# A rotation stage that sums its squares with tokens on partitions, inverts 128x32 roots and turns them back

## What is computed

```
def rms_norm(x, w):
    xf = x.astype(jnp.float32)
    y = xf * lax.rsqrt(jnp.mean(xf * xf, axis=-1, keepdims=True) + EPS)
    return (y * w.astype(jnp.float32)).astype(x.dtype)
...
    out = jnp.concatenate([x1 * cos - x2 * sin, x2 * cos + x1 * sin], axis=-1)
...
        q = rope(rms_norm(q.reshape(B, S, N_HEADS, HEAD_DIM), q_norm_w[l]), pos)
        k = rope(rms_norm(k.reshape(B, S, N_KV_HEADS, HEAD_DIM), k_norm_w[l]), pos)
```

## Time and profile before

| what | value |
|---|---|
| median of 3 runs | 3251.81 us (3251.74 to 3253.85) |
| the profiled execution's own time | 3248.22 us |
| its span in the trace | 3246.2 us |
| TensorE busy (PE) | 3004.8 us, 93% |
| weight loads (PEld, beside PE) | 2370.2 us, 73% |
| VectorE (DVE) | 2255.4 us, 69% |
| ScalarE (ACT) | 1640.5 us, 51% |
| mean granted clock of TensorE | 0.976 of full speed |
| the stage of the change | 1774.7 to 2310.6 us |

### The profile page before, as it was taken

How to read it: one execution, slowest core, us unless ns; L and a number is a source line. 1 busy time by engine, 2 the same in 40 slices (tenths; PEclk the granted TensorE clock), 3 DMA queues, 4 the chain that set the end, 5 groups by cost and what they waited for, 6 DMA issues and landing times. The chain is left out here.

```text
span 3246.2 us, 48173 instructions
## 1 busy us (share of the span) xinstructions
PE 3004.8 (93%) x17460; PEld 2370.2 (73%) x17460; DVE 2255.4 (69%) x3296; ACT 1640.5 (51%) x3004; POOL 195.0 (6%) x448
## 2 busy tenths in 40 slices
PE   6999999999998989999999999999777889998799
PEld 5888788888787767777777778776655666776587
DVE  8888877754667758888876645324378789988543
ACT  5443422233545437777778232112377788888400
POOL 0000000000000000110000000000022111212100
PEclk8999999999999999999999999999889999999899
DMA  4444422245566541111155343223721111011665
GB/s 119 117 115 124 138 70 65 85 143 160 149 201 212 177 135 37 50 31 31 44 166 170 87 130 107 94 84 100 191 46 33 27 24 24 21 37 44 151 189 156
DMA packets 377861, 331.48 MB, mean 102 GB/s; under 512 B 100989, under 2 KB 331901, under 8 KB 371473
## 3 DMA queue, kind: packets, MB, share of 16 engines
q1 hardware_dynamic: 371640, 292.35, 31.7%
q0 software_dynamic: 5264, 35.72, 3.0%
q10 hardware_dynamic: 720, 0.31, 0.0%
HBM read 211.26 MB, written 107.10 MB: 98 GB/s over the span
## 5 line engine op out<-in xcount | busy, mean ns | idle before, releaser
L629 PE MATMUL p_oa_acc<-s_h_a_hi,s_mx_w_hi 128*128 128x512 f32 x768 | 301.7, 393 | 15.8 <-DVE s_h_a_lo L418 9.4
L323 ACT ACTIVATE s_mx_w_hi<-s_mx_raw 128x512 fp32r<-128x512 f32 x224 | 139.0, 629 | 320.6 <-PE p_oa_acc L629 256.8
L629 PE MATMUL p_oa_acc<-s_h_a_lo,s_mx_w_hi 128*128 128x512 f32 x768 | 300.0, 391 | 0.0
L629 PE MATMUL p_oa_acc<-s_h_a_hi,s_mx_w_lo 128*128 128x512 f32 x768 | 299.9, 390 | 0.0
L1598 DVE TENSOR_TENSOR_SCAN s_st_prod<-s_st_soft,s_st_prod 128x512 f32<-128x512 f32 x192 | 234.4, 1268 | 15.8 <-ACT s_st_soft L1525 15.8
L3123 PE MATMUL p_sa_turn<-s_ident,s_sa_arg 128*128 128x128 f32 x1088 | 167.4, 290 | 58.6 <-ACT s_sa_prob L2751 34.9
L1525 ACT ACTIVATE s_st_soft<-p_st_z 128x512 f32<-128x512 f32 (+3 forms) x320 | 153.7, 534 | 111.0 <-PE p_st_z L1650 111.0
L2340 PE MATMUL p_pr_ps<-s_h_hi,s_pr_w_hi 128*128 128x512 f32 (+1 forms) x712 | 195.0, 394 | 10.6 <-ACT s_pr_stage L2187 8.8
L3123 PEld LDWEIGHTS p_sa_turn<-s_ident,s_sa_arg 128*128 128x128 f32 x1088 | 120.7, 145 | 100.1 <-issue 61.7
L460 DVE TENSOR_TENSOR s_mx_w_lo<-s_mx_raw,s_mx_w_hi 128x512 fp32r<-128x512 f32 x224 | 153.4, 685 | 57.7 <-ACT s_mx_w_hi L323 56.1
L2340 PE MATMUL p_pr_ps<-s_h_lo,s_pr_w_hi 128*128 128x512 f32 (+1 forms) x712 | 192.9, 392 | 0.0
(11 more groups left out here) (376 smaller groups left out, 7375.4 us busy)
## 6 DMA issues: line engine op xcount, KB each, us to landing
s_mx_raw<-in_w_in_a SPq DMA_DIRECT2D x128, 256.0 KB, 3.9
s_pb_ada<-in_w_ada SPq DMA_DIRECT2D x16, 768.0 KB, 4.3
s_pr_raw<-in_w_in SPq DMA_DIRECT2D x21, 512.0 KB, 3.9
s_pr_work<-s_pr_stage SPq DMA_DIRECT2D x38, 256.0 KB, 4.8
d_rot_hi<-s_pr_rot POOLq DMA_DIRECT2D x9, 1024.0 KB, 4.3
d_rot_lo<-s_pr_stage POOLq DMA_DIRECT2D x9, 1024.0 KB, 6.2
d_p_t<-s_pr_stage POOLq DMA_DIRECT2D x9, 1024.0 KB, 8.2
d_y_t<-s_mx_y SPq DMA_DIRECT2D x16, 512.0 KB, 5.7
```

The source lines that it names most:

```text
L323: nc.scalar.activation(w_hi[:, m], raw[g % 2][:, m], ACT.Copy).then_inc(hi_done, 1)
L629: ins = nc.tensor.matmul(bank, w[:, m, k, :], a[:, m, k, :], start=(k == 0 and n == 0), stop=(k == KH - 1 and n == 2))
```

## The change

The squares are now the stationary operand: for each of the 16 tiles of 128 tokens, one matmul with a 128x2 matrix of zeros and ones (`of_head`) as moving operand gives, with tokens on partitions, the sums of the two heads: 128x32 in all. ScalarE takes the root of these 32 columns into `root`, VectorE their reciprocal into `rinv`, then copies it, each value 64 times side by side, into `wide` (tokens by channels). 16 transposes (`spread_back`) turn that back to channels by tokens in the norm block's PSUM tile, where the last product of `rotate` reads it. The sums move from k-slice 3 to k-slice 2 of the next block; the transposes stand before k-slice 5. TensorE may overwrite the tile only behind `posted`. The squares may overwrite `wide` once the previous norm block is summed (`summed`), no more once it is posted. The reciprocal is no longer counted in the chain semaphore; its own semaphores `rinv_done`, `inverted` and `spread` order it.

```diff
 def wide_free(eng, b):
...
             if before and before[-1] in norms_of:
-                eng.wait_ge(posted, posts[before[-1]] + 1)
+                eng.wait_ge(summed, norms_of[before[-1]] + 1)
...
         @block.gpsimd
-            nc.gpsimd.memset(ones[:], 0.0).then_inc(ones_ready, 1)
+            nc.gpsimd.memset(of_head[:], 0.0).then_inc(ones_ready, 1)
             pool.wait_ge(ones_ready, 2)
             for h in range(2):
-                nc.gpsimd.memset(ones[h * HD:h * HD + HD, h * HD:h * HD + HD], 1.0).then_inc(ones_ready, 1)
+                nc.gpsimd.memset(of_head[h * HD:h * HD + HD, h:h + 1], 1.0).then_inc(ones_ready, 1)
...
             def behind(b):
                 if b in norms_of:
                     act.wait_ge(summed, norms_of[b] + 1)
-                    nc.scalar.activation(wide[:], ps[b % 2][:], ACT.Sqrt, bias=eps[:], scale=1.0 / HD).then_inc(rooted, 1)
+                    nc.scalar.activation(root[:].rearrange("p t h -> p (t h)"), ps[b % 2][:, 0:2 * TILES], ACT.Sqrt, bias=eps[:], scale=1.0 / HD).then_inc(rooted, 1)
...
-                a, s, r = halves(stage[0:rows, b % 2]), work[0:rows, :, 0:HALF], halves(wide[0:rows])
+                a, s, r = halves(stage[0:rows, b % 2]), work[0:rows, :, 0:HALF], halves(ps[b % 2][0:rows])
...
                 dve.wait_ge(rooted, norms_of[b] + 1)
-                nc.vector.reciprocal(wide[:], wide[:]).then_inc(done, 1)
-                count[0] += 5
+                nc.vector.reciprocal(rinv[:], root[:]).then_inc(rinv_done, 1)
+                dve.wait_ge(rinv_done, norms_of[b] + 1)
+                nc.vector.tensor_copy(wide[:].rearrange("p (t h d) -> p t h d", h=2, d=HD), rinv[:].unsqueeze(3).to_broadcast([P, TILES, 2, HD])).then_inc(inverted, 1)
+                count[0] += 4
                 dve.wait_ge(done, count[0])
                 then(nc.vector.tensor_tensor(a, a, s, ALU.add))
+                dve.wait_ge(spread, norms_of[b] + 1)
                 nc.vector.tensor_tensor(a, a, r, ALU.mult).then_inc(posted, 1)
...
             def sum_squares(b):
                 pe.wait_ge(squared, norms_of[b] + 1)
-                for t in range(NT):
-                    ins = nc.tensor.matmul(ps[b % 2][:, t * 512:t * 512 + 512], ones[:], wide[:, t * 512:t * 512 + 512], start=True, stop=True)
+                for t in range(TILES):
+                    ins = nc.tensor.matmul(ps[b % 2][:, 2 * t:2 * t + 2], wide[:, t * P:t * P + P], of_head[:], start=True, stop=True)
                 ins.then_inc(summed, 1)
+
+            def spread_back(b):
+                pe.wait_ge(inverted, norms_of[b] + 1)
+                for t in range(TILES):
+                    ins = nc.tensor.transpose(ps[b % 2][:, t * P:t * P + P], wide[:, t * P:t * P + P], ident[:])
+                ins.then_inc(spread, 1)
...
                 if b - 2 in norms_of:
-                    pe.wait_ge(rooted, norms_of[b - 2] + 1)
+                    pe.wait_ge(posted, posts[b - 2] + 1)
...
-                    if k == 3 and b - 1 in norms_of:
+                    if k == 2 and b - 1 in norms_of:
...
+                    if k == 5 and b - 1 in norms_of:
+                        spread_back(b - 1)
```

More of the change, by code:

```diff
@@ L2008, in load_keys, with phase_project_rotate @@
             sp.dma_start(lo[rows, cols].bitcast(F32), rot_lo[row:row + HD, cols]).then_inc(landed, 16)
-def phase_project_rotate(nc, sem, w_in, xt_hi, xt_lo, w_pool, pool_scale, cos_t, sin_t, inv_count, p_t, mix_t, rot_hi, rot_lo, space, first, first_ps):
+def phase_project_rotate(nc, sem, w_in, xt_hi, xt_lo, w_pool, pool_scale, cos_t, sin_t, inv_count, p_t, mix_t, rot_hi, rot_lo, ident, space, first, first_ps):
     HALF = SEQ // 2
@@ L2064, in phase_project_rotate @@
         eps = al.sb("pr_eps", [P, 1])
-        ones = al.sb("pr_ones", [P, P])
+        of_head = al.sb("pr_of_head", [P, 2])
+        root, rinv = (al.sb("pr_" + of, [P, TILES, 2]) for of in ("root", "rinv"))
         ps = [first_ps, al.ps("pr_ps1", [P, SEQ])]
@@ L2069, in phase_project_rotate @@
         const_in, ones_ready, done, xs_in = sem("pr_const_in"), sem("pr_ones_ready"), sem("pr_chain"), sem("pr_xs_in")
-        squared, summed, rooted = sem("pr_squared"), sem("pr_summed"), sem("pr_rooted")
+        squared, summed, rooted, rinv_done, inverted, spread = sem("pr_squared"), sem("pr_summed"), sem("pr_rooted"), sem("pr_rinv"), sem("pr_inverted"), sem("pr_spread")
         posted, mixed, blended = sem("pr_posted"), sem("pr_mixed"), sem("pr_blended")
@@ L3354, in program @@
                 phase_project_rotate(nc, sem, a["w_in_2"][0], *xt, a["w_pool_2"][0], a["pool_scale_2"][0],
-                                     a["cos_t"], a["sin_t"], a["inv_count"], p_t, mix_t, rot_hi, rot_lo, space, out_space, first_ps)
+                                     a["cos_t"], a["sin_t"], a["inv_count"], p_t, mix_t, rot_hi, rot_lo, ident, space, out_space, first_ps)
             space.before_selection(Alloc(nc, third))
```

## The result

The changed kernel's median is 3263.61 us (3258.44 to 3270.45, 6 runs), that of the kernel before, in as many runs, 3251.77 us. The ratio is 1.0038, with a 95% interval of 1.0028 to 1.0047: 12 us slower (9 to 15). The profiled execution took 3258.44 us, the shortest of the six, 10.2 more than the profiled one of before; the prediction's sum for it was 3256.4.

The account below looks back on a forecast made before the run. TensorE was taken to set the pace in the rotation stage. The terms 0.3 + 8.9 - 5.5 + 4.5 = +8.2 us, added to the runs' median of 3251.81, gave 3260.0 us; range 3254 to 3270.

Parts of the forecast that it names:

- the forecast's own case: Rotation stage: the summed terms hold, +8.2 us, with its own range of +5 to +10 us; chance 0.50.
- signs of being wrong: Passes at 0.06 or 0.2 us, 1.2 GHz behind sums, waits before every block's transposes, gains in pool blocks or next stage.
- Part 1, the sums: TensorE's sums of squares: 32 passes at 0.11 us, 3.5 us a sum; five sums +0.3 us.
- the not-slower rival: Sums at k = 2: passes of 0.06 us make each sum 1.9 us; in all +0.1, no difference; chance 0.12.
- that of the open loads: Narrow sums: weight loads lie open, a pass takes 0.19 us; +13, in all +21 us; chance 0.08.
- Part 2, the transposes: Transposes back on TensorE: sixteen take 1.77 us; five times, +8.9 us.
- Part 3, the stalls: TensorE's waits for the squares before sums: the short reciprocal gets the store done in time, all 5.5 us come back.
- Part 4, the new wait: TensorE at k = 5 waits for spread reciprocals: 3.1 us in block 0, 1.4 in block 8; together +4.5 us.
- Block 8's swapped rows: Rival: rows 1.9 us late also in blocks 2, 4 and 6; each stalls 1.4 us, in all 12.4; chance 0.10.
- the forecast's lower price: Spreading copy at 1227 ns by the skill: the two stalls would be 2.0 and 0.3 us, the sum below 5.9.
- The clock: Rival: array on 2 columns taken for idling, clock falls, each sum costs 1.6 us more: +8, in all +16; chance 0.20.

Follow-up runs that it names:

- run 6: Changed kernel with its narrow sums scattered behind products of k-slices 2 and 3, and 1 transpose in place of 16; ratio to the kernel before 0.9992.
- run 3: Changed kernel with its 16 narrow sums set one behind each of the first 16 products of k-slices 2 and 3; ratio to the kernel before 1.0021.
- run 5: Kernel before, with the reciprocal over only the first 32 of 2048 columns; ratio to the kernel before 0.9981.
- run 1: Changed kernel with the 16 narrow sums replaced by 4 calls of 512 moving columns, identity as weights; ratio to the kernel before 1.0021.
- run 4: Kernel before, with its sums of squares set before k-slice 4 in place of 3; ratio to the kernel before 0.9991.
- run 7: Kernel before, with VectorE making a rotated block's low part ahead of the next weights' low part; ratio to the kernel before 0.9978.
- run 8: Kernel before, with the low part first and the sums of squares in fp32r; median 3234.61 us, ratio to the kernel before 0.9946.
- run 2: Changed kernel with 1 transpose in place of 16 before k-slice 5, narrow sums still in one run; ratio to the kernel before 1.0029.
- run 9: Changed kernel, unaltered, profiled once more; one execution, 3266.68 us, stage 544.4 us.
- run 10: Changed kernel with narrow sums in one run and 1 transpose in place of 16, profiled a second time; one execution, stage 542.2 us.

## Why the prediction came out as it did

The direction and the range (3254 to 3270) hold, and the likeliest time, 3260.0, is 3.6 us off; the measured 3263.61 lies just outside the 3257 to 3262 of the forecast's own case. Its sum does not hold term by term. Two errors of like size cancelled, a wait that did not come (+4.5) and a fallen clock that was left out of the sum (+4.8), so the nearness of the total is luck. Of the prediction's own signs of being wrong one came true: stretches of 1.2 GHz behind the sums.

*Part 1, the sums.* A pass of 0.11 us was right (3.5 us a sum; +0.7 in all where +0.3 was forecast). With it the not-slower rival and that of the open loads are both out: the passes kept the pace of the earlier trace rows, neither 0.06 nor 0.19 us.

*Part 2, the transposes.* Right: 1.77 us for the 16 of a block, 8.9 in all; run 6 against run 3 shows 15 of the 16 worth 8.6 us in the stage, and some 9 by the ratios.

*Part 3, the stalls.* Right: run 5 has them gone by the shorter reciprocal alone, worth 5 to 6 us; 5.9 were lost and 5.5 priced.

*Part 4, the new wait.* This step failed: +4.5 us were forecast and none came. Half of the error is the copy, taken from the wrong neighbour: it is 1227 ns, not 2290. The copy reads one source, L2296 two. The Trainium skill ("VectorE: DVE Perf Modes", "The perf-mode tier table") gives 1227 ns for an fp32 copy of this size, and the trace agrees. Block 8's swapped rows, late before, were on time here (8.9 us behind leave, as in the others). In block 0 a wait of 1.1 us, where the forecast's lower price was 2.0, shows in run 1; in the changed kernel TensorE arrived late itself, because the clock had fallen.

*The clock.* This rival had 0.20, and its mechanism is what happened, in three of five sums (four in the second profile): +4.8 us, not +8. What I held against it was no argument. Weights were loaded throughout here too: the loads were busy 3.56 of 3.60 us in the stretch above. And the sums of before, which no fall had followed, streamed 512 columns a pass. With the falls in, the lower price of the copy and no stall, the sum is 0.7 + 8.9 - 5.9 + 4.8 = 8.5; the stage measured 8.9 and the profiled execution 10.2. The medians are 11.8 apart. Over all executions the changed kernel lost 6 to 9 us more to the clock than the one before (93.0 against 87 and 84), with an error of 4. With that in place of the 4.8 the sum is 10 to 13, so the other executions may well lose the rest to the clock too. In which stage is not shown.

The Trainium skill ("TensorE: Matmul & The Clock Gate", Part 1, "What's actually happening") says that a hardware monitor sets the array's clock by how busy the array has been of late. The fall of run 4, behind a stretch with TensorE busy 1.35 of 3.40 us, agrees with that. The falls at the narrow sums do not settle it: by the trace's records TensorE was busy 3.60 of 3.60 us ahead of block 0's.

Not tried: passes of more than 2 and fewer than 512 columns in one run, and narrow passes without new weights.

## What to carry to other kernels

On an engine that sets the pace, price a change by that engine first: here VectorE was relieved of 58 us, TensorE was given 9, and the 6 us that it won back were to be had by moving one instruction ahead of another (run 7). A run of matmuls with a few moving columns can cost more than its own time, here 1.6 us for 3.5 in most of the sums; scattered among wide ones they cost only their own. Sums over partitions that feed a norm can take fp32r operands where their rounding is tolerable: in run 8 they took half the passes at half the time each, 0.94 us in place of 3.5.

## What was not expected

With work left out the clock was worse: with 15 transposes fewer a block, TensorE spent 27.3 us of the norm blocks at 1.2 GHz in place of 10.2, in both profiles alike, and the gain of 8.3 us was lost there. That the missing transposes are the cause is not shown. And the falls come at narrow sums in one run: at 17 of 20 such sums (the changed kernel and runs 2, 9 and 10), and at 0 of 15 that were wide or scattered beside the same transposes or one (runs 1, 3 and 6). Of the 25 wide sums without transposes (the kernel before and runs 4, 5, 7 and 8) one had a fall, the one in run 4 that came behind a wait of 2.0 us.
